# A decoder layer with a mixture of experts on one core: a new order of the expert tiles, and expert loads issued by the count at which their slot comes free

## What is computed

```python
def expert_block(args):
    xblk, e = args
    return (jax.nn.silu(xblk @ w_gate[e]) * (xblk @ w_up[e])) @ w_down[e]
```

## Time and profile before

| | |
|---|---|
| median of 3 runs | 1073.52 us |
| profiled execution | 1071.9 us |
| its span, first to last instruction | 1070.2 us |
| mean granted TensorE clock | 0.953 |
| PE busy | 951.8 us (89%) |
| VectorE busy | 658.4 us (62%) |
| ScalarE busy | 460.0 us (43%) |
| GpSimd busy | 337.3 us (32%) |
| q1, the queue of SP's loads: share of the 16 DMA engines over the span | 56.1% |
| q0, the queue of GpSimd's gathers and scatters | 7.3% |

### The profile page before, as it was taken

The page is one execution under the profiler, slowest core; times in us unless marked ns, Lnnn a source line. Parts: engine busy times, 40 slices in busy tenths (PEclk is TensorE's granted clock), DMA queues, the critical chain, the costliest instruction groups (busy, mean ns, idle before and its releaser), DMA issues.

```text
span 1070.2 us, 12147 instructions
## 1 busy us (share of the span) xinstructions
PE 951.8 (89%) x4533; PEld 683.2 (64%) x4533; DVE 658.4 (62%) x745; ACT 460.0 (43%) x555; POOL 337.3 (32%) x254
## 2 busy tenths in 40 slices
PE   7999999999999996699998898899877989999930
PEld 5758888787788885575643564465325778888820
DVE  5569999798777677756310530431004989999842
ACT  6675446434732223345201320321104677777650
POOL 0277998822210001113211221031111433333243
PEclk9999999999999997699999899999998999999975
DMA  9520202200353226769799799979999999999662
GB/s 321 164 80 1 79 1 79 62 18 1 115 201 116 82 99 250 259 249 383 247 394 417 268 385 400 415 248 396 419 412 417 381 402 388 407 389 391 243 247 88
DMA packets 65438, 265.23 MB, mean 248 GB/s; under 512 B 10932, under 2 KB 29556, under 8 KB 40800
## 3 DMA queue, kind: packets, MB, share of 16 engines
q1 hardware_dynamic: 51792, 237.07, 56.1%
q0 software_dynamic: 10176, 18.87, 7.3%
q10 hardware_dynamic: 3408, 8.48, 2.0%
HBM read 249.44 MB, written 29.37 MB: 261 GB/s over the span
## 4 chain that ended last, share of the span: by engine, by line
PE 33%; DMA 22%; DVE 3%; issue 2%; ACT 1%; POOL 1%; SPq 0%; POOLq 0%; ACTq 0%; DVEq 0%
PE ps L2207 8%; PE ps L2209 8%; PE ps L2208 8%; DMA raw_b<-in_expert_w_down_dram 5%; DMA raw_b<-in_expert_w_up_dram 4%; DMA raw_b<-in_expert_w_gate_dram 3%; PE ps L2234 3%; PE ps L2247 3%; DMA raw<-in_expert_w_up_dram 2%; DMA raw<-in_expert_w_gate_dram 2%; PE ps L2200 2%; DMA summed_rows<-ym,idx_g 1%; DMA summed_rows<-ym,idx_h 1%; DMA sums<-summed_rows 1%; ACT hi_a L1204 1%
## 5 line engine op out<-in xcount | busy, mean ns | idle before, releaser
L2207 PE MATMUL ps<-hi_a,xm_hi 128*128 128x512 f32 x304 | 126.0, 415 | 5.3 <-DVE lo_a L1764 2.8
L820 POOL DMA_INDIRECT summed_rows<-ym,idx_g x25 | 61.4, 2457 | 208.5 <-DVE ym L1813 201.1
L2234 PE MATMUL ps<-raw,xm 128*64 128x512 f32 x256 | 115.0, 602 | 13.7 <-DMA raw_b<-in_expert_w_up_dram 9.9
L2209 PE MATMUL ps<-hi_a,xm_lo 128*128 128x512 f32 x304 | 124.2, 409 | 0.0
L2234 PE MATMUL ps<-raw_b,xm 128*64 128x512 f32 x256 | 115.2, 603 | 4.1 <-DMA raw<-in_expert_w_up_dram 4.1
L1764 DVE TENSOR_TENSOR lo_a<-raw,hi_a 128x2048 fp32r<-128x2048 f32 x32 | 72.6, 2287 | 65.1 <-ACT hi_a L1204 64.9
L1376 DVE SCALAR_TENSOR_TENSOR ps<-uT,pcol,ps 128x1024 f32<-128x1024 f32 (+1 forms) x87 | 96.5, 1109 | 2.4
L731 POOL TENSOR_TENSOR acc<-x,acc 128x1024 f32<-128x1024 f32 x30 | 85.3, 2843 | 29.0 <-ACT x L996 24.9
L1764 DVE TENSOR_TENSOR lo_b<-raw_b,hi_a 128x2048 fp32r<-128x2048 f32 x28 | 63.5, 2288 | 35.5 <-ACT hi_a L1204 35.5
L805 POOL DMA_INDIRECT xg<-hf_rows,idx_g x27 | 28.7, 1062 | 177.3 <-PE ps L2200 152.6
L1204 ACT ACTIVATE hi_a<-raw 128x2048 fp32r<-128x2048 f32 x32 | 60.8, 1915 | 45.8 <-PE ps L2247 20.5
(11 more groups left out here) (355 smaller groups left out, 2324.0 us busy)
## 6 DMA issues: line engine op xcount, KB each, us to landing
raw_b<-in_expert_w_gate_dram SPq DMA_DIRECT2D x32, 1024.0 KB, 16.2
raw_b<-in_expert_w_up_dram SPq DMA_DIRECT2D x32, 1024.0 KB, 17.0
raw<-in_expert_w_up_dram SPq DMA_DIRECT2D x32, 1024.0 KB, 17.2
raw<-in_expert_w_gate_dram SPq DMA_DIRECT2D x32, 1024.0 KB, 14.0
raw_b<-in_expert_w_down_dram SPq DMA_DIRECT2D x32, 1024.0 KB, 20.1
raw<-in_expert_w_down_dram SPq DMA_DIRECT2D x32, 1024.0 KB, 17.4
raw<-in_w_in_dram SPq DMA_DIRECT2D x8, 1024.0 KB, 7.1
xa<-in_x_dram SPq DMA_DIRECT2D x8, 512.0 KB, 8.8
```

Source lines behind the costliest of these rows:

```text
L820: return pool.indirect_dma_start(out=sum_dram, out_offset=bass.IndirectOffsetOnAxis(ap=at.bitcast(U32), axis=0), in_=src, in_offset=None, ...
L2207: pe.matmul(dst, x_hi, w_h, start=first, stop=False)
L2209: return pe.matmul(dst, x_lo, w_h, start=False, stop=stop)
L2234: last = pe.matmul(ps[r * BL:(r + 1) * BL, i // 2, :], xm[:, kk, r * BL:(r + 1) * BL], slot(n, i)[:, w], start=(kk == 0), stop=(kk == KC - 1))
```

## The change

Two things change. `KINDS` becomes SS, three rounds of DEPSPSS, then PPSS: the same 27 tiles with the same kinds (3 D, 3 E, 13 S, 8 P), in another order. And SP's loads no longer follow the tiles. They are sorted by the value of `split_used` at which their slot comes free, and among equals by first use. Each load keeps its wait.

```diff
--- before.py
+++ after.py
@@ -54,7 +54,7 @@
     N_D, N_S, N_P = 3, 11, 8
     N_DYN = NE - FIXED
     assert N_DYN == N_D + N_S + 2 * N_P
-    KINDS = "SS" + "PDEP" + "PDEP" * 2 + "PP" + "S" * 11
+    KINDS = "SS" + "DEPSPSS" * 3 + "PPSS"
     NS = len(KINDS)
     N_IDX = FIXED + 2 * N_D + N_S + N_P
     N_TILE = N_IDX - FIXED
@@ -500,6 +500,14 @@
 
             return split_used, after_piece(tile_of(n), i)
 
+        def first_use(n, i):
+
+            t = min(t for t, places in enumerate(tile_pos) if n in places)
+            return 6 * t + 5 + i if i >= 4 else 6 * t + i
+
+        load_order = sorted(((n, i) for n in range(FIXED, NE) for i in range(6)),
+                            key=lambda p: (slot_free(p[0] - 2, p[1])[1], first_use(*p), p))
+
         split_no, hi_before, n_split, was = {}, {}, 0, None
         for t, kind in enumerate(KINDS):
             if kind in "SD":
@@ -621,23 +629,13 @@
             load_expert(1, 5, 1)
 
             who = {}
-
-            def load_part(t, parts):
-                for i in parts:
-                    for n in tile_pos[t]:
-                        sp.wait_ge(*slot_free(n - 2, i))
-                        load_expert(n, i, who[n])
-
             sp.wait_ge(order_rdy, 1)
-            for t in range(FIXED, NS):
-                if KINDS[t] != "E":
-                    for n in tile_pos[t]:
-                        r = rank_at[n]
-                        who[n] = sp.value_load(order[0:1, r:r + 1], min_val=0, max_val=NE - 1)
-                    load_part(t, range(4))
-                if t > FIXED and KINDS[t - 1] != "E":
-                    load_part(t - 1, (4, 5))
-            load_part(NS - 1, (4, 5))
+            for n, i in load_order:
+                if n not in who:
+                    r = rank_at[n]
+                    who[n] = sp.value_load(order[0:1, r:r + 1], min_val=0, max_val=NE - 1)
+                sp.wait_ge(*slot_free(n - 2, i))
+                load_expert(n, i, who[n])
 
             def load_sums():
                 for t in range(NT):
```

## The result

The changed kernel took 1081.74 us (median of 9 runs, 1078.65 to 1085.35) and the kernel before 1075.08 us (9 runs on the same chip, 1068.78 to 1078.81). The ratio is 1.0063, with a 95% interval of 1.0041 to 1.0085: some 6.7 us slower. The forecast was 16.6 us slower, 1090 us. The sign was right, the size was over twice too large. The profiled execution took 1083.07 us, with a span of 1081.3 us and a clock of 0.948.

A forecast was written before the change was run, and what follows sets the result against it. From 470 us the stage was taken to last as long as its DMA work plus idle troughs, where PE isn't longer; +9.6 us in the stage and +7 at the end gave 1088.5 and, as median, 1090 us; range 1068 to 1108.

The forecast's parts named there:

- So a stretch of the stage lasts as long as its DMA work and its troughs: Expert stage, where PE isn't longer: a round is 140.3 us of DMA work plus 11 us idle, 151.3 us.
- Each round is 3.2 us longer: Each of three DEPSPSS rounds takes 151.3 us, where the same seven tiles took 148.1 us before.
- After two S tiles the queue is a little ahead, and I take 78: Tiles P, P, S behind the rounds take 78 us, where three such tiles took 84.3 us before.
- I take +7: End: the sums wait for two scatters in a row, 18.6 us, not one of 8.21; +7, between 0 and +10.4 us.
- some 17 us later: Sign expected in the changed profile: the sums loaded some 17 us later than at 1013.6 us.
- Reason behind the troughs: D and E: the large expert holds six slots for two tiles, only six pieces enter the queue; 11 us idle per round.
- Rival 1: With nine or more pieces queued at D's first product, the troughs close: rounds of 140.3 us, 1057 us; chance 0.13.
- Rival 2: The bytes decide: troughs of 7.8 us per round as before, the end covered, 1074 us within 5 us; chance 0.12.
- Rival 3: Stalls on VectorE's order at seven steps from a pair, 4.4 us each outside the DMA's time: 1115 us; chance 0.18.
- The order of loads ... fills part of the old troughs: Sorted loads: SP never waits for a slot while another is free, filling part of the old troughs; no size given.
- My own bounds: Idle of 5 us per round (1072) to 15 us (1102); 0 or +10.4 us at the end moves them by -7 or +3.

The follow-up runs named there:

- e6: The changed kernel with E tiles multiplying by stand-in operands, so the large expert's slots come free with D; ratio to the kernel before 1.0074.
- e2: The changed kernel's tiles (DEPSPSS three times, PPSS) with the old tile-by-tile order of loads; ratio to the kernel before 1.0298.
- e3: The changed kernel with rounds PPDESSS in place of DEPSPSS, both pairs ahead of D, sorted loads; ratio to the kernel before 0.9966.
- e4: The changed kernel with rounds DEPPSSS in place of DEPSPSS, both pairs behind E, sorted loads; ratio to the kernel before 1.0165.
- e13: e3 with the last pairs one tile earlier: PPDESSS twice, PPDESS, PPSSS; ratio to the kernel before 1.0020.
- e8: The changed kernel's sorted loads with tiles SS, PPDEP, DEP, PDEP, nine S, PPSS; ratio to the kernel before 0.9967.
- e16: e8 with VectorE waiting until the first scatter of pairs 2, 9, 13, 23 and 24 is issued; ratio to the kernel before 0.9972.

## Why the prediction was right and wrong

- **"So a stretch of the stage lasts as long as its DMA work and its troughs".** Held for the first two rounds: 150.6 us (482.90 to 633.54) and 151.1 us (633.54 to 784.60), where 151.3 were predicted. Idle DMA time in the quoted windows is 6.6 + 2.2 = 8.8 us in the second round and 7.8 + 2.8 = 10.6 us in the third, near the 11 predicted. The places are right too: one trough in D, one in the pair behind E. For the first round the match is in part luck: its windows from 480 to 530 us show 14 us idle.
- **"Each round is 3.2 us longer", times three.** This is the first term that was mis-sized. The third round took 147.6 us (to 932.21), 3.7 less than its term. Its last load landed 139.7 us after the round's first product, where the other two took 142.0 and 142.4, and from there to the next product it was 7.9 us in place of 8.7. It is the one that a pair follows, not a D tile. Why that shortens it was not tested. Against the 3 x 148.1 us that I had worked out for before, the rounds cost 5.0 us and not 9.6.
- **"After two S tiles the queue is a little ahead, and I take 78".** This is the second. It took 75.4 us (6.9 + 1000.71 - 932.21), 2.6 less. With the 4.6 us of the rounds (0.7, 0.2 and 3.7) this makes the 7.2 us by which the stage came out shorter than the sum: 5.0 - 2.6 = +2.4 in place of +9.6. The stage's term was mis-sized, though each piece of it was within 4 us: a small difference of large sums.
- **"I take +7" at the end.** Measured +5.4 to the load of the sums, 5.9 with what follows. Mechanism right: two scatters in a row, 7.59 and 5.32 us, where the loaded ones that I took were 7.39 and 10.42. The second was issued in 2.17 us and not 2.98, and the DMA share around them was 0.73 (1010 to 1020 us), where it was 1.01 around my row of 10.42 (840 to 850 us). That sums would be loaded "some 17 us later" counted both terms; it was 10.6 us, 2.8 of them the front's.
- **Reason behind the troughs.** "The large expert keeps its six slots for two tiles, so few slots come free" counted the slots rightly: two down and four gate and up pieces were issued from 15.2 to 29.6 us after D's first product (648.70 to 663.1 against 633.54), and +15.0 to +29.5 was said. But it named the wrong cause. e6 freed them 18 us sooner for no gain. What e6's timeline shows in its place is that all twelve slots were full of unused pieces.
- **Rival 1**, the troughs close: wrong, the share fell to 0.24 to 0.36. **Rival 2**, the bytes decide: wrong, since the interval excludes no change, though the result is a little nearer to its 1074 (7.7 us) than to my 1090 (8.3 us). **Rival 3**, stalls on VectorE's order: wrong, 1.9 us for 13.3, though there were seven such steps and not four.
- **"The order of loads ... fills part of the old troughs"** was left without a price, as if it could not matter much. With these tiles it is worth 25 us (e2). Part of that is blocked issue, part a mechanism that I didn't have, the long scatter. The changed kernel has two of 7.81 us itself, but no wait of PE hangs on them. The trace of before had it in small: the issue that takes 1.62 us at 1028.48 took 3.51 in the S run and 5.61 at 878.77, and I passed over it.

The changed kernel is thus slower by two terms of the sum: some 2.4 us in the stage, where the rounds' troughs outweigh what the last pairs gain, and 5.9 us at the end, where the third tile from the end is now a pair. The forecast's range of 1068 to 1108 held the time. My own bounds make 1072 - 7 = 1065 to 1102 + 3 = 1105; the stated range is not quite their sum.

## What to carry to other kernels

A transfer queue that runs dry isn't mended by freeing a buffer sooner when all the buffers are full of unused data: count what can be ahead, and try to put the work that uses no new data where the queue is full as it begins. e3, with the pairs ahead of D, took 145.6 us for its first round and the changed kernel 150.6. Price the order of issue together with the order of work, since the same edit was worth nothing here and 25 us there. And when an issue on GpSimd shows several durations for the same operation, look at once at what VectorE does beside it, above all where the end of the program hangs on that issue. Compare versions with their long issues counted, too, or the chance of one is taken for the worth of an order, as it nearly was in e4. One wait of VectorE behind one instruction took 6 us off e13.

## What the runs showed of the hardware

A split here is a float32 TENSOR_TENSOR of VectorE with both operands in SBUF, 2.29 us long. The twenty profiles hold 674 scatters of GpSimd from 470 us on.

- With no split running as it starts, a scatter is issued in 1.4 to 1.7 us, also where a split begins just behind it (e13: 1.59 us at 857.98, a split 0.13 us later). Three at the end of the program took 1.95 to 2.60 us beside another operation of VectorE, that on `sums`.
- With a split running, it ends 1.3 to 1.5 us behind the end of that split, even where the next follows without a gap. That is the 3.5 us of the S run, as at 896.68 us of the kernel before: the split that began at 896.40 ends at 898.69, the scatter at 900.19.
- 34 scatters took longer, 5.6, 7.7 to 7.8 or 9.9 to 10.0 us. All of them had a split that began 0.32 to 0.39 us ahead of them. In e2 the one of tile 6 ended at 625.84 us, 1.4 us behind the last split of the run of four (624.49). In the changed kernel, at 639.43 us, it took 7.81 us and ended 1.5 us behind the last of three (645.75), with no wait of PE behind it. 14 others with such a start took 3.3 to 3.5 us. Tile 14 of e8 and of e16 is such a couple: 3.41 us at 793.77 and 10.02 us at 794.22, each with a split begun 0.36 to 0.37 us ahead and more behind it. What decides between them the traces don't show.

VectorE's operations with an operand in PSUM (`hm`, `xm_lo`) follow the splits, and the scatter ends beside them.

The Trainium skill, page "SBUF — State Buffer", section "A bandwidth-pool intuition that's wrong (but worth ruling out)", describes the like for a copy of VectorE: descriptors that GpSimd can't write until VectorE gives a shared port back, with a DMA of some 620 ns that took some 3100 ns beside one copy. The runs agree in kind, with another VectorE operation: most of the scatters that meet a running split wait for the end of that one split. In the 34 long ones they differ, since the scatter got its turn only behind two to four splits.
